# Three rounded passes for the first mixers' output projection, and expert loads of up to four chunks

## The reference

```python
a = pool_mixer(z_pool, ...) @ w_branch_pool
b = short_conv_mixer(z_c, z_b, z_v, ...) @ w_branch_conv
m = sigmoid(gate_a) * a + sigmoid(gate_b) * b      # (256, 1024), the merged branches
x = x + m @ w_out                                  # the output projection that is changed
h2 = rmsnorm(x, g_ffn)
x = x + peer_ffn(h2, w_q, sub_keys, expert_u, expert_v)   # 8 heads x 16 gathered experts a token
```

```python
for gi in range(4):    # w_gate, w_up: (8, 1024, 512) a group; w_down: (8, 512, 1024)
    hg = silu(einsum('nd,edf->nef', x, wg[gi])) * einsum('nd,edf->nef', x, wu[gi])
    y = y + einsum('nef,efd->nd', hg * gates[:, gi, :, None], wd[gi])
```

## Time and profile before

| | us |
|---|---|
| median of 3 runs | 1974.74 (1971.47 to 1975.72) |
| the profiled execution, its own time | 1972.88 |
| its span | 1971.0 |
| PE busy in the span | 1622.6 (82%) |
| DVE, ACT, POOL busy | 994.2, 551.1, 611.7 |
| DMA | 633.81 MB, mean 322 GB/s |

### The profile page before, as it was taken

How to read it: one execution, slowest core, us unless ns; L and a number is a source line. 1 busy time by engine, 2 the same in 40 slices (tenths; PEclk the granted TensorE clock), 3 DMA queues, 4 the chain that set the end, 5 groups by cost and what they waited for, 6 DMA issues and landing times.

```text
span 1971.0 us, 22005 instructions
## 1 busy us (share of the span) xinstructions
PE 1622.6 (82%) x8676; PEld 1026.2 (52%) x8676; DVE 994.2 (50%) x1898; ACT 551.1 (28%) x959; POOL 611.7 (31%) x396
## 2 busy tenths in 40 slices
PE   7799986777777777778999999999999966666665
PEld 7696842232222223326999988987895411212211
DVE  7573866886778775544573895554434200000001
ACT  4342421212222212114443546445631100000001
POOL 3441734444445444434573205443320000000000
PEclk9999999999999999999999999999999988788878
DMA  8756599999999999994544433544489999999997
GB/s 336 308 195 239 207 394 421 421 421 422 422 421 421 422 421 418 421 406 155 172 145 166 150 129 128 188 171 150 158 352 383 400 426 425 426 425 426 425 425 320
DMA packets 83869, 633.81 MB, mean 322 GB/s; under 512 B 10008, under 2 KB 12824, under 8 KB 15408
## 3 DMA queue, kind: packets, MB, share of 16 engines
q1 hardware_dynamic: 42624, 353.39, 45.4%
q0 software_dynamic: 36864, 268.45, 32.9%
q10 hardware_dynamic: 4272, 10.50, 1.6%
HBM read 631.23 MB, written 1.07 MB: 321 GB/s over the span
## 4 chain that ended last, share of the span: by engine, by line
DMA 44%; PE 41%; DVE 9%; ACT 2%; issue 2%; POOL 0%; ACTq 0%; SPq 0%; DVEq 0%; POOLq 0%
DMA t<-in_expert_uv,t 21%; PE ps L623 5%; PE ps L628 5%; PE ps L625 5%; DMA t<-in_eu 4%; DMA ring<-in_ed 4%; PE ps L687 4%; PE ps L700 3%; DVE t L2137 3%; PE ps L831 3%; PE ps L834 2%; DMA t<-in_eg 2%; PE ps L643 2%; PE ps L644 2%; PE ps L649 2%; DMA g<-in_ed 2%
## 5 line engine op out<-in xcount | busy, mean ns | idle before, releaser
L196 POOL TENSOR_TENSOR t<-ring,t 128x1024 fp32r<-128x1024 f32 x125 | 317.9, 2556 | 469.0 <-ACT t L188 468.8
L831 PE MATMUL ps<-t 128*128 128x512 f32 x444 | 241.4, 626 | 141.9 <-ACT t L1469 141.9
L2813 POOL DMA_INDIRECT t<-in_expert_uv,t x222 | 247.9, 1117 | 321.7 <-PE ps L834 290.8
L2137 DVE CUSTOM_DVE_ANT_0 t<-t 128x1024 f32<-128x1024 f32 x222 | 273.0, 1235 | 138.6 <-DMA t<-in_expert_uv,t 136.5
L188 ACT ACTIVATE t<-ring 128x1024 fp32r<-128x1024 f32 x220 | 230.3, 1054 | 215.6 <-PE ps L628 70.7
L834 PE MATMUL ps<-t 128*128 128x512 f32 x444 | 230.1, 600 | 0.0
L831 PEld LDWEIGHTS ps<-t 128*128 128x128 f32 x444 | 77.2, 192 | 284.9 <-ACT t L1469 227.2
L196 DVE TENSOR_TENSOR t<-ring,t 128x1024 fp32r<-128x1024 f32 x95 | 139.9, 1480 | 126.6 <-ACT t L188 123.8
L1143 PE MATMUL ps<-t 128*32 128x512 f32 x816 | 123.5, 725 | 71.4 <-DMA t<-in_eg 26.4
L623 PE MATMUL ps<-t 128*128 128x256 f32 x1120 | 163.0, 288 | 14.7 <-ACT t L188 9.1
L1462 ACT ACTIVATE t<-t 128x2 f32<-128x2 f32 x129 | 26.2, 203 | 497.8 <-DVE t L2137 497.4
(11 more groups left out here) (393 smaller groups left out, 2034.0 us busy)
## 6 DMA issues: line engine op xcount, KB each, us to landing
ring<-in_w_in SPq DMA_DIRECT2D x82, 1024.0 KB, 4.9
t<-in_eg SPq DMA_DIRECT2D x12, 2048.0 KB, 35.0
t<-in_eu SPq DMA_DIRECT2D x11, 2048.0 KB, 41.0
t<-in_ed SPq DMA_DIRECT2D x11, 2048.0 KB, 38.7
ring<-in_ada_w SPq DMA_DIRECT2D x20, 1024.0 KB, 7.7
ring<-in_eg SPq DMA_DIRECT2D x9, 2048.0 KB, 38.8
ring<-in_eu SPq DMA_DIRECT2D x8, 2048.0 KB, 36.4
t<-in_ed SPq DMA_DIRECT2D x14, 1024.0 KB, 37.0
```

The costliest lines, as they stand in the source:

```text
L196: e.tensor_tensor(p.lo, p.view, p.hi.bitcast(F32), ALU.subtract).then_inc(self.w.lo[eng], 1)
L831: ins = e.matmul(sums[tt][0], s.diag[col % 4], v[:, 1024:1536], start=first, stop=last)
L2137: ins = e.tensor_tensor_reduce(out=g[:, 0:1024], in0=g[:, 0:1024], in1=s.hN[:, col // 128, :], scale=1.0, scalar=0.0, op0=ALU.mult, op1=AL ...
L2813: m.gathered[s.place[col]].up(e.indirect_dma_start(out=s.gb[col], out_offset=None, in_=m.a_in["expert_uv"], in_offset=bass.IndirectOffsetO ...
```

## The change

Three edits go together.

1. The first mixers' output projection runs in three passes. Its weights become 8 parts whose rests POOL makes. PE takes column half 0 for both token tiles (`pe_rows`), then column half 1 for tile 0 and for tile 1 (`pe_rows_tile`). The merged branches are split pair by pair: ACT rounds each pair of blocks (new, 4 instructions), DVE subtracts (`lo`, 4 instructions) and raises `rests`, for which PE waits before each of the first four parts. Tile 0 is turned after tile 1's last matmul.
2. The expert matrices lie in HBM as one array `ew` in the order of use, so that neighbouring chunks of two matrices are neighbours in memory too. Up to `TOGETHER = 4` chunks in neighbouring slots make one DMA (32 KB a partition). The slots' order is changed: `wide`'s eight form two runs of four, and `x` and `g12` lie side by side.
3. The four `ada_w_2` chunks of the last stage use other slots of `wide` and are issued behind two chunks of expert weights.

The diff, cut to what is spoken of:

```diff
+MATRICES = [("eg", 0), ("eu", 0)] + [(name, n) for q in range(8) for name, n in (("eg", q + 1), ("eu", q + 1), ("ed", q)) if n < 8]
+TOGETHER = 4
...
-    s.wo = [[m.w.raw(src) for src in halves(a["w_out"][n])] for n in range(2)]
+    s.sp.expect([src for n in range(2) for src in halves(a["w_out"][n])], "G", "rows")
...
-    ring_e = cqk + rest[:2] + [m.extra] + rest[2:] + oct_ + [more] + [ring[i] for i in turn] + [m.g12, hT, x_t[:, :]]
-    home = ([(wide, 0), (wide, 1), (wide, 4), (wide, 5), None, (wide, 6), (wide, 7), (wide, 2), (wide, 3), None]
-            + [(ring_t, i) for i in turn] + [None] * 3)
-    late, begun = range(4), 10 + RING
-    o.w = Weights(ring_e, sem, "_e", False, late, [*range(4, len(ring_e) - 3), *late, *range(len(ring_e) - 3, len(ring_e))])
+    slots = rest + [m.extra] + cqk + oct_ + [more] + [ring[i] for i in turn] + [m.g12, hT, x_t]
+    home = ([(wide, 4 + i) for i in range(4)] + [None] + [(wide, i) for i in range(4)] + [None]
+            + [(ring_t, i) for i in turn] + [(xg_t, 1), None, (xg_t, 0)])
+    ada = [0, 1, 2, 3]
+    begun = ada + [*range(4, 10 + RING), *ada, 10 + RING, 11 + RING, 12 + RING]
+    freed = {5: "ra", 6: "ra", 7: "oc", 8: "oc", **{n: "mod" for n in range(10 + RING, 14 + RING)}}
+    o.w = Weights(slots, sem, "_e", False, begun, [*range(4, 10 + RING), *ada, 11 + RING, 12 + RING, 10 + RING])
...
+    for c, d in zip(o.w.chunks[len(ada):-8], o.w.chunks[len(ada) + 1:-8]):
+        tile, at = home[c.slot] or (None, 0)
+        lead, old = c.lead, d.n < len(begun)
+        if (len(lead.group) < TOGETHER and tile is not None and home[d.slot] == (tile, at + 1)
+                and (not old or c.n in freed and freed[c.n] == freed.get(d.n))):
+            d.lead = lead
+            lead.group.append(d)
+            first, n = at + 1 - len(lead.group) + 1, len(lead.group) * HALF
+            start = 8 * HALF * (len(MATRICES)) - (len(o.w.chunks) - lead.n) * HALF
+            lead.joined = tile[:, first * HALF:first * HALF + n], a["ew"][:, start:start + n]
...
-def pe_rows(m, e, sp, key, xs):
+def pe_rows(m, e, sp, key, xs, ready=None):
...
+        if ready is not None:
+            e.wait_ge(*ready.turn("pe"))
...
-    e.wait_ge(*m.merged.turn("pe"))
-    run(pe_raw_out(m, e, "wo1", s.mT, s.wo, 0))
+    run(pe_rows(m, e, s.sp, ("wo1", 0), s.hT, m.rests))
+    parts = []
+    pe_rows_tile(m, e, s.sp, ("wo1", 1), s.hT, 0, parts)
     pe_mod_row(m, e, 7, s.mod4[1])
-    for step, _ in enumerate(pe_raw_out(m, e, "wo1", s.mT, s.wo, 1)):
-        if step == 2:
-            pe_turn_tile(m, e, "hT2", r3(m.hold, 2)[:, 0, :], 0, m.normed)
+    pe_rows_tile(m, e, s.sp, ("wo1", 1), s.hT, 1, parts)
+    pe_turn_tile(m, e, "hT2", r3(m.hold, 2)[:, 0, :], 0, m.normed)
...
     act_mod(m, e, s, 7)
     act_mod_row(m, e, s, 6)
-    for tt in range(2):
-        e.wait_ge(*b.taken(("wo1", tt, 1)))
+    for q in range(4):
+        e.wait_ge(*m.merged.turn("act"))
+        m.high.up(e.activation(s.hT[0][:, 2 * q:2 * q + 2, :], s.mT[:, 2 * q:2 * q + 2, :], ACT.Copy))
+    for q in range(5):
+        s.sp.take(e, "act")
+    for tt in range(2):
+        e.wait_ge(*b.taken(("wo1", 1, tt)))
         act_norm(m, e, m.x, s.pf_f, (tt,))
+        for q in range(2 - tt):
+            s.sp.take(e, "act")
         if tt == 0:
             act_mod_row(m, e, s, 7)
...
+    def lo(q):
+        h, l = (t[:, 2 * q:2 * q + 2, :] for t in s.hT)
+        e.wait_ge(*m.high.turn("dve"))
+        m.rests.up(e.tensor_tensor(l, s.mT[:, 2 * q:2 * q + 2, :], h.bitcast(F32), ALU.subtract))
...
-            dve_gated(m, e, ("br", br, q), s.mT, 2 * q, s.sg[:, 2 * q:2 * q + 2, :], s.tmp, br == 0, q == 3)
+            if br and q:
+                e.wait_ge(m.merged.sem, m.merged.n)
+            dve_gated(m, e, ("br", br, q), s.mT, 2 * q, s.sg[:, 2 * q:2 * q + 2, :], s.tmp, br == 0, br == 1)
+            if br and q:
+                lo(q - 1)
...
+    lo(3)
     dve_bias4(m, e, 7)
-    for tt in range(2):
-        for n in range(2):
+    for n in range(2):
+        for tt in range(2):
             xs = m.x[:, tt, n * 512:n * 512 + 512]
-            e.wait_ge(*b.full(("wo1", tt, n)))
-            b.emptied(e.tensor_tensor(xs, xs, b.ap(("wo1", tt, n)), ALU.add), ("wo1", tt, n))
-            if tt and n == 0:
+            e.wait_ge(*b.full(("wo1", n, tt)))
+            b.emptied(e.tensor_tensor(xs, xs, b.ap(("wo1", n, tt)), ALU.add), ("wo1", n, tt))
+            if n == 0:
+                continue
+            if tt:
                 dve_tile_lo(m, e, "hT2", *m.s2.hT, 0)
-        dve_norm(m, e, m.x, m.grow[1], r3(m.hold, 2), (tt,))
+            dve_norm(m, e, m.x, m.grow[1], r3(m.hold, 2), (tt,))
...
-    load(e, we, 0, 2)
+    load(e, we, 5, 7)
     e.wait_ge(*b.full(("oc", 3, 1)))
-    load(e, we, 2, 4)
-    load(e, we, 5, 7)
+    load(e, we, 0, 4)
...
-    load(e, we, at + 3, 194)
+    load(e, we, at + 3, m.s4.count)
...
+        "ew": np.concatenate([experts[name][q] for name, q in MATRICES], axis=1),
```

More of the change, by code:

```diff
@@ L316, in lay_out @@
     sig("norm_sum", "norm_ms", "norm_root", "normed", "high", "ones", "stage_end", "silu_c", "csg", "fours")
-    sig("pools", "pool_hi", "conv_y", "conv_hi", "conved", "merged")
+    sig("pools", "pool_hi", "conv_y", "conv_hi", "rests", "merged")
     sig("index", "diff", "expo", "dotted", "gelu", "weighted", "diag", "fin_a", "fin_sq", "fin_ms",
@@ L539, in lay_out @@
     m.mod.update({n: [o.w.raw(src) for src in halves(a["ada_w_2"][n])] for n in (10, 11)})
[L540 to L552, removed]
-    o.w.recount()
+    column = {key: 8 * n * HALF for n, key in enumerate(MATRICES)}
+    o.at = {(name, q): [(o.w if q or k > 1 or name != "eg" else o.w0).raw(a["ew"][:, n:n + HALF])
+                        for k in range(8) for n in (column[name, q] + k * HALF,)] for name, q in MATRICES}
+    for c, d in zip(o.w.chunks[len(ada):-8], o.w.chunks[len(ada) + 1:-8]):
[8 more added lines that the diff above has]
+            lead.joined = tile[:, first * HALF:first * HALF + n], a["ew"][:, start:start + n]
+    o.count = len(o.w.chunks)
     o.dense = {}
@@ L779, in pe_mixers1 @@
         else:
-            e.wait_ge(*m.conved.turn("pe"))
+            e.wait_ge(*m.rests.turn("pe"))
         for q in range(4):
@@ L1094, in pe_retention @@
         pe_mod_sum(m, e, n, r.mod4[n - 8])
-    e.wait_ge(*m.merged.turn("pe", 2))
+    e.wait_ge(*m.merged.turn("pe", 6))
     wo = [s.wo[0:2], s.wo[2:4]]
@@ L1681, in gate @@
     def gate(n):
-        free = m.merged.turn("act", 2) if n == 0 else ()
+        free = m.merged.turn("act") if n == 0 else ()
         run(act_cols(m, e, s.sp, ("gate2", "c", n), s.sg, n, ACT.Sigmoid, free=free))
@@ L2860, in load @@
             continue
-        for d in (c, c.mate):
-            if d and d.before:
+        for d in c.group:
+            if d.before:
                 if d.before.picked is None:
@@ L2866, in load @@
                     given_back(e, m, d.before)
-        e.dma_start(*(c.both or (c.ap, c.src))).then_inc(w.landed[c.slot], 16)
+        e.dma_start(*c.joined).then_inc(w.landed[c.slot], 16)
 def load_bias(m, e):
@@ L2913, in sync_program @@
     load(e, we, at + 2, at + 3)
-    load(e, we, at + 3, 194)
+    load(e, we, at + 3, m.s4.count)
     e.wait_ge(m.counted.sem, 1)
     with e.If(e.value_load(m.s4.many[0:1, 0:1], min_val=0, max_val=256) > SLOTS):
-        load(e, we, 194, len(we.chunks))
+        load(e, we, m.s4.count, len(we.chunks))
     e.wait_ge(m.fin_row.sem, 2)
@@ L3011 @@
     cst, masks = constants()
+    experts = {
+        "eg": fours(i["expert_w_gate_2"][0].reshape(8, 4, 8, 128, 512)),
+        "eu": fours(i["expert_w_up_2"][0].reshape(8, 4, 8, 128, 512)),
+        "ed": fours(i["expert_w_down_2"][0].reshape(8, 4, 4, 128, 2, 512).transpose(0, 1, 4, 2, 3, 5).reshape(
+            8, 4, 8, 128, 512)),
+    }
     arrays = {
```

22 lines of the change are left out of this document (9 added, 13 removed).

## The result

The changed kernel took 1978.6 us (median of 20 runs, 1971.6 to 1983.0), the kernel before 1974.1 in as many. The ratio is 1.0024, 95% interval 1.0017 to 1.0031: slower by 4.7 us, where 1971.6 was forecast and 1977 was the upper end. The profiled execution took 1981.0, its span 1979.2 against 1971.0.

What follows compares the result with a forecast made beforehand. PE was taken to bound the first mixers up to head 0, DMA transfers the gathers and experts. Terms +0.5 (projection), -4.3 (packets), +0.7 (expert start) gave -3.1 us, so 1971.6 us as median, range 1967 to 1977.

Steps and rivals of the forecast that it cites:

- the one on the clock: PE behind the 2.2 us gap before the projection: half clock makes first parts some 1.7 longer, hidden by POOL's chain.
- The start: PE's first projection matmul waits for ACT's rounding and DVE's rest of the merged pair: 2.2 us lost.
- The matmuls: First mixers' projection on PE: 96 matmuls at 0.227 us each, 21.8 us in place of 27.87.
- GpSimd as the bound of the middle: Projection's weight splits: ACT rounds the fourth part from 167.2, POOL's five parts end at 181.1, PE waits for them.
- The turning exposed: After the projection PE waits out tile 0's turning and split, formerly hidden by the last four matmuls: 2.4 us.
- Head 0's start: Head 0's query columns on PE start at 190.3 against 190.62 before, plus 0.8 for DVE and POOL colliding.
- The shared port: Tile 0's norm on DVE may wait for a POOL part: 0.8 us taken, bounds 0 and 4.8.
- rival D: Port lock between DVE and POOL holds the first mixers' chain: parts of 3.07, whole +6.0, 1980.7 us; chance 0.10.
- Edit 1 in sum: The first mixers' projection change as a whole: -0.3 + 0.8 = +0.5 us, bounds -4.3 and +9.
- The packets: Expert loads: 11.7 ns a packet, fewer packets with four-chunk loads, 4.3 us less.
- 0.7 lost at the start: Start of the expert stage: second load waits for four chunks, 1.5 later, of which 0.8 is covered; loss 0.7 us.
- The load of chunks 17 to 20 is issued 1.7 later as well: Expert load issued 1.7 us later, into the stretch that ends in the idle time at 1530; costs nothing.

Runs made afterwards that it cites:

- e4: The changed kernel with GpSimd's first three query-weight parts waiting until the tiles' norms are multiplied; 1977.2 us, ratio 1.0018 to the kernel before.
- e3: The changed kernel with PE transposing the identity matrix in all three new waits, before and after the projection; 1974.9 us, ratio 1.0007 to the kernel before.
- e5: The changed kernel with identity transposes on PE only in the waits after the projection, around tile 0's turning and before head 0; 1975.3 us, ratio 1.0008.
- e2: The kernel before with the second and third edits alone (one expert array, loads of up to four chunks, slot order); 1971.8 us, ratio 0.9994.
- e1: The kernel before with the first edit alone (first mixers' output projection in three passes), expert loads as before; 1983.7 us, ratio 1.0054.

## Why the prediction was wrong, point by point

- **The step that failed** is the one on the clock: "At half speed the first parts take some 1.7 longer, but POOL's chain holds the end, and hides it." I asked it only of the wait that the edit makes ahead of the projection. There the half clock came in two of five profiles with this wait open, and GpSimd's chain hid little of it. Of some 1.5 us that PE lost on its matmuls (the second L671 starts 13.6 behind the first L648, 12.0 in the second profile), 0.9 arrives at head 0 (32.1 against 31.1 to 31.3), since PE at full clock had waited only 0.31 for GpSimd. Where it counts I didn't ask at all. I had written down 2.4 us of idle PE behind the turning three paragraphs earlier, and behind it PE is the chain up to head 0's scores and nothing covers it. Half clock there costs 3.0 to 5.5 us to the picks, and 5 to 6 to the first gather. Rows 8 showed both outcomes behind gaps of about 2.5, so it belonged in the range with 5 us and a chance.
- The start: 2.2 forecast, 2.43 measured. Right.
- The matmuls: 0.227 each forecast, 12 in 2.81 in a full stretch measured, 0.235: 0.7 us too little.
- GpSimd as the bound of the middle: nearly right. The sum counts from a row at 159.91, which began at 158.94. On its scale ACT starts the fourth part at 167.0 (167.2 forecast) and GpSimd ends the fifth at 180.3 (181.1 forecast), as a part took 2.42 and the bias row didn't delay them. PE waited 0.3 for them where its clock was full at 162, and not in the changed kernel's first profile, where it was late itself.
- The turning exposed: 2.4 forecast; 3.4 from its start to head 0, 0.8 of it the collision (2.6 in e4).
- Head 0's start: 190.3 + 0.8, or 31.2 behind the row; measured 31.1 to 31.3 with the full clock at 162. Here the sum was right, with the matmuls' pace a little too fast and GpSimd's parts a little too slow.
- The shared port: the collision came as in rival D, in both tiles, 2.1 us a pair. The Trainium skill (page SBUF — State Buffer, section Who interferes with whom) says that a DVE instruction with two SBUF inputs and a GpSimd one that reads SBUF contend, and that whoever issues first keeps the shared port pair for its whole instruction while the other waits. The trace agrees, with 3.55 against 1.41 beside a part of 2.4. On the way to head 0 the term was 0.8 to 0.9 (e4), the 0.8 that I took as half of 1.6, by luck: PE had slack, and tile 1's meeting was hidden. That the same kind of meeting among the picks delays the first gather (two there before, up to four in the changed kernel, 0.8 to 2.1 us) stood nowhere in the sum.
- Edit 1 in sum: +0.5 forecast. With the clock held up (e3, e5) it is +0.2 to +0.8 against the profile of before and +0.9 to +1.5 against e2's; pairs whose picks took equally long (e3 and e2, e5 and before) give +0.8 to +0.9. With the half clock +6.
- The packets: 11.7 ns was right as engine time and wrong as time of the stage, 8.5 by the rate: 41 x 144 / 16 x 8.5 = 3.1 us instead of 4.3. The fit took both queues of the earlier trace rows at the same 100.7%; within one queue the share moves with the packets. With 0.7 lost at the start, 2.4 would have been the forecast, and e2 shows 2.0 by the medians and 1.2 by the ratio (-0.4 to 3.0). The 10.5 ns that stands beside it in the prediction (the Trainium skill, page DMA: Bandwidth & Descriptors, section Bandwidth) is there the shortest time of a transfer of 64 packets, divided by 64, and not a price on one of 16 engines in a full queue: that it lies near 11.7 confirms nothing.
- "The load of chunks 17 to 20 is issued 1.7 later as well ... it costs nothing" holds: the idle time at 1530 is gone (0.95 above), and in the 160 us that end 60 behind the experts' first product 60.8 MB move in both profiles of the changed kernel, 61.1 and 60.8 in before and e1: at most 0.3 MB less, 0.7 us.
- The chances: D had 0.10, the right side and a time near the measured one, but that is luck. Its lock came, but its price didn't: the parts took 2.42 and not 3.07, and the collisions of the norms cost 0.8 to 0.9 and not 6.6. With the clock asked at each new wait, slower would have had about 0.4, as I judge it now.

## What to carry to other kernels

When an edit leaves PE a new wait on the critical chain, price the work behind the wait at half clock too, not only the wait: here 2.1 us idle cost another 5 to 6 up to the next stage. A test is cheap: put transposes into the wait and see whether the time falls. And a gain in matmuls doesn't arrive while the rounding and the splits that they need stand behind other work on ACT and GpSimd; move these first, then count, and follow the chain on to the engine that has the next stage, here DVE, whose picks grew by 0.8 to 2.1 us as GpSimd's parts moved.
